# Norm statistics as wide products with a mean matrix, and products into a free bank before the first tile of each norm

## The reference

```python
def rms_norm(x, g):
    y = x * lax.rsqrt(jnp.mean(x * x, axis=-1, keepdims=True) + EPS)   # EPS = 1e-6
    return y * g

def modulate(h, shift, scale):
    return h * (1 + scale) + shift
```

## Time and profile before

| | |
|---|---|
| median of 3 runs | 3732.96 us (3728.23 to 3733.44) |
| profiled execution | 3734.95 us, span 3733.2 us |
| TensorE busy | 3505.1 us, 94% of the span |
| VectorE busy | 1916.7 us, 51% |
| ScalarE busy | 1265.7 us, 34% |
| GpSimd busy | 373.7 us, 10% |
| granted TensorE clock, mean | 0.966 of full |

### The profile page before, as it was taken

The page is one execution under the profiler, slowest core; times in us unless marked ns, Lnnn a source line. Parts: engine busy times, 40 slices in busy tenths (PEclk is TensorE's granted clock), DMA queues, the critical chain, the costliest instruction groups (busy, mean ns, idle before and its releaser), DMA issues.

```text
span 3733.2 us, 40477 instructions
## 1 busy us (share of the span) xinstructions
PE 3505.1 (94%) x17064; PEld 2896.1 (78%) x17064; DVE 1916.7 (51%) x2662; ACT 1265.7 (34%) x1779; POOL 373.7 (10%) x216
## 2 busy tenths in 40 slices
PE   2999999899979999999999999989999998999998
PEld 2888888788767888788777888766788876678887
DVE  8433343566656453635344333486564538656464
ACT  4322122444433222322234222334342432344242
POOL 3311001111110000000001000420100033010001
PEclk9999999899989999999999999989999999999999
DMA  5423241011115353535212232210232222012221
GB/s 193 141 80 123 85 152 63 29 35 35 34 63 174 124 198 113 190 122 176 89 66 96 92 101 96 82 53 6 68 106 97 96 74 75 6 52 98 99 96 57
DMA packets 95798, 348.83 MB, mean 93 GB/s; under 512 B 10624, under 2 KB 11136, under 8 KB 95104
## 3 DMA queue, kind: packets, MB, share of 16 engines
q1 hardware_dynamic: 94320, 343.06, 27.6%
q10 hardware_dynamic: 1296, 3.18, 0.2%
HBM read 344.10 MB, written 2.10 MB: 93 GB/s over the span
## 4 chain that ended last, share of the span: by engine, by line
PE 84%; DVE 9%; ACT 4%; POOL 1%; issue 1%; DMA 0%; SPq 0%; ACTq 0%; DVEq 0%; POOLq 0%
PE PS L341 83%; DVE CAC L1872 2%; ACT G L1111 1%; DVE ST L1679 1%; PE PS L413 1%; DVE WL L1448 1%; POOL SM L2160 1%; DVE SCR L1479 1%; ACT HH L994 1%; ACT G L982 1%; DVE PTL L1662 1%; DVE X L1843 0%; ACT PTH L1092 0%; DVE ST L1963 0%; DVE SCR L1471 0%
## 5 line engine op out<-in xcount | busy, mean ns | idle before, releaser
L341 PE MATMUL PS<-HH,WH 128*128 128x512 f32 (+1 forms) x3120 | 1194.4, 383 | 46.8 <-DVE HL L1560 21.1
L341 PE MATMUL PS<-HL,WH 128*128 128x512 f32 (+1 forms) x3120 | 1177.9, 378 | 0.0
L341 PE MATMUL PS<-HH,WL 128*128 128x512 f32 (+1 forms) x3120 | 1174.6, 376 | 0.0
L1448 DVE TENSOR_TENSOR WL<-RAW,WH 128x1024 fp32r<-128x1024 f32 x462 | 580.9, 1261 | 895.3 <-ACT WH L943 895.2
L943 ACT ACTIVATE WH<-RAW 128x1024 fp32r<-128x1024 f32 x496 | 523.2, 1057 | 1217.2 <-PE PS L341 1206.9
L341 PEld LDWEIGHTS PS<-HH,WH 128*128 128x128 f32 x3120 | 595.4, 191 | 164.0 <-DVE HL L1560 23.3
L341 PEld LDWEIGHTS PS<-HL,WH 128*128 128x128 f32 x3120 | 595.3, 191 | 109.4 <-issue 5.5
L341 PEld LDWEIGHTS PS<-HH,WL 128*128 128x128 f32 x3120 | 594.0, 190 | 108.7
L341 PE MATMUL PS<-AH,WH 128*128 128x512 f32 x1392 | 525.9, 378 | 1.7 <-DVE WL L1448 1.7
L341 PE MATMUL PS<-AL,WH 128*128 128x512 f32 x1392 | 525.5, 377 | 0.0
L341 PE MATMUL PS<-AH,WL 128*128 128x512 f32 x1392 | 523.8, 376 | 0.0
(11 more groups left out here) (277 smaller groups left out, 3288.2 us busy)
## 6 DMA issues: line engine op xcount, KB each, us to landing
RAW<-wst SPq DMA_DIRECT2D x640, 512.0 KB, 3.3
X<-xT SPq DMA_DIRECT2D x1, 2048.0 KB, 12.2
out<-X SPq DMA_DIRECT2D x8, 256.0 KB, 2.0
PTF<-cb SPq DMA_DIRECT2D x1, 1024.0 KB, 4.8
Y<-yT SPq DMA_DIRECT2D x1, 1024.0 KB, 6.9
PTF<-cb ACTq DMA_DIRECT2D x1, 1024.0 KB, 4.8
HM<-sg ACTq DMA_DIRECT2D x4, 256.0 KB, 3.7
ROPE<-rope SPq DMA_DIRECT2D x1, 512.0 KB, 4.5
```

Source lines behind the costliest of these rows:

```text
L341: return e.matmul(o, l, r, start=start, stop=stop)
L1448: e.tensor_tensor(lo, raw_block(s), f32(hi), ALU.subtract).then_inc(*did("dve_done", ("wlo", b)))
```

## The change

A constant column of 1/1024 (CST column 643), broadcast to 128x128, is the stationary matrix `mean`. A wide fp32 product of it with a tile of 512 or 768 tokens leaves the mean over the features on all 128 partitions at once. `means` issues such products, adding up in a bank:

- The one of ACC is put inside the last projection's tile m = 7, before its last input but one (`squares`). For f01 POOL adds only the squares of m = 1 to 3, and TensorE sums ACC and the other four. The one of G follows after m = 7, and after it `busy` issues three products with ROPE, a constant table, into a bank that nobody reads (bank 7, at f01 bank 1; none at f00).
- ACT takes the square root from the bank into ACC, with 1e-6 added; DVE takes the reciprocal on 128x512 or 128x768; DVE multiplies X by the gain column and by ACC in one instruction into G; ACT adds the bias and writes HH directly; DVE makes HL from G, bias and HH in one instruction. The POOL powers of the norms are gone.
- For layer norms `center` puts the product for the provisional mean before input 5 of tile m = 6 (4 in a mixer's projection), that of A2t before input 5 of m = 7, those of X(6) and ACC before input 10 (7 in a mixer's projection). DVE shifts X(6) before its own eviction. After m = 7 follow X(7), G, and four products with ROPE. ACT squares and copies the mean, DVE makes the variance, ACT the root, DVE the reciprocal; POOL subtracts the mean from X(1) to X(7) (1 to 5 at the end), which DVE did before.
- `prepare` loads the ACT tables early: 27 loads in the program.

The diff, cut to its core:

```diff
+        def means(name, src, N, step, start, stop, *more, into=None):
+
+            if start:
+                _, prior = take(name, N) if into is None else hold(name, N, into)
+                for p in prior:
+                    q.wait_ge(*p)
+            q.wait_ge(*step)
+            for c in range(0, N, 512):
+                d = min(c + 512, N)
+                m = mm(bank[name][:, c:d], mean, src[:, c:d], start, stop)
+            if stop:
+                more = ("tile", name), *more
+            if more:
+                m.then_inc(*did("pe_done", *more))
+
+        def busy(st, n):
+
+            bk, prior = hold(("busy", st), NX, 1 if st == "f01" else 7, ("busy", st))
+            for p in prior:
+                q.wait_ge(*p)
+            for i in range(n):
+                m = mm(bk, mean, ROPE[:, 0:512], True, True)
+            m.then_inc(*did("pe_done", ("busy", st)))
...
+        def squares(st):
+
+            up = BEFORE[st]
+            q.wait_ge("consts")
+            means(("ms", st), ACC, tokens(st), ("acc", up, 3 if up == "at" else 6), True, False, ("acc read", st),
+                  into=0 if up == "at" else 6)
+
         def norm(st):
-            up = BEFORE[st]
-            nt = 6 if wide(up) else 4
-            q.wait_ge("consts")
-            stat(st, [(ACC, 128, ones, ("acc", up, 6)), (G(("sq", up, 7)), 128, ones, ("sq", up, 7))], nt, 1,
-                 ("gdone", ("sq", up, 7)))
-            spread(st, nt, None, ("rs", st))
-            N = nt * 128
+            up, N = BEFORE[st], tokens(st)
+            for m in range(4, 8) if up == "at" else (7,):
+                means(("ms", st), G(("sq", up, m)), N, ("sq", up, m), False, m == 7, ("gdone", ("sq", up, m)))
+            if st != "f00":
+                busy(st, 3)
             return [(*hview(k, N), ("h", st, k), 128) for k in range(8)]
...
+        def center(st, m, at):
+
+
+            up = BEFORE[st]
+
+            def first():
+                means(("mean", st), ACC, NX, ("sum", st), True, True)
+
+            def second():
+                means(("v", st), A2t, NX, ("csq", st, 3), True, False, ("a2 read", st), into=7)
+
+            def third():
+                means(("d", st), X(6), NX, ("x", up, 6), True, False, into=6)
+                means(("v", st), ACC, NX, ("csq", st, 6), False, False, ("acc read", st))
+
+            return {6: {(at[0], 0): first}, 7: {(at[1], 0): second, (at[2], 0): third}}.get(m, {})
 
         def layer_norm(st):
...
+            means(("d", st), X(7), NX, ("x", BEFORE[st], 7), False, True)
+            means(("v", st), G(("ce", st, 7)), NX, ("csq", st, 7), False, True, ("gdone", ("ce", st, 7)))
+            if st != "end":
+                _, prior = hold(("busy", st), NX, 5, ("busy", st))
                 for p in prior:
                     q.wait_ge(*p)
+                for i in range(4):
+                    m = mm(bank["busy", st], mean, ROPE[:, 0:512], True, True)
+                m.then_inc(*did("pe_done", ("busy", st)))
             return [(*hview(k, NX), ("h", st, k), 128) for k in range(8)]
...
+            e.activation(ACC[:, 0:N], bank["ms", st][:, 0:N], ACT.Sqrt, bias=EP[:, 0:1]).then_inc(
+                *did("act_done", ("std", st), ("free", ("ms", st))))
+                a = e.activation(hi[:, 0:512], s[:, 0:512], ACT.Identity, bias=mcol(l, 3 * i, k, 0))
+                    a = e.activation(hi[:, 512:768], s[:, 512:768], ACT.Identity, bias=mcol(l, 3 * i, k, 1))
+                a.then_inc(*did("act_done", ("hhi", st, k)))
+                    part(upto[LAST[st]], 1)
...
+            q.wait_ge("tile", ("d", st))
+            q.wait_ge("a2 read", st)
+            e.activation(A2t[:, :], bank["d", st][:, :], ACT.Square).then_inc(*did("act_done", ("dsq", st)))
+            q.wait_ge("acc read", st)
+            e.activation(ACC[:, 0:512], bank["d", st][:, :], ACT.Copy).then_inc(*did("act_done", ("dcopy", st)))
+            q.wait_ge("var", st)
+            q.wait_ge("eps")
+            e.activation(A2t[:, :], A2t[:, :], ACT.Sqrt, bias=EP[:, 1:2]).then_inc(*did("act_done", ("std", st)))
...
+            q.wait_ge("std", st)
+            e.reciprocal(ACC[:, 0:N], ACC[:, 0:N]).then_inc(*did("dve_done", ("rs", st)))
+            q.wait_ge("rs", st)
+            spans = [(X, 0, 512, "x")] + ([(Y, 512, 768, "y")] if N > 512 else [])
+            for k in range(9):
+                    for s, (src, c, d, kind) in enumerate(spans):
+                        q.wait_ge(kind, up, k)
+                        e.scalar_tensor_tensor(out=G(use)[:, c:d], in0=src(k), scalar=mcol(l, 3 * i + 1, k, s), in1=ACC[:, c:d], op0=ALU.mult,
+                                               op1=ALU.mult).then_inc(*did("dve_done", ("nx" if d == N else "nxx", st, k)))
+                if k:
+                    use = ("n", st, k - 1)
+                    hi, lo = hview(k - 1, N)
+                    q.wait_ge("hhi", st, k - 1)
+                    for s, (src, c, d, kind) in enumerate(spans):
+                        e.scalar_tensor_tensor(out=lo[:, c:d], in0=G(use)[:, c:d], scalar=mcol(l, 3 * i, k - 1, s), in1=f32(hi)[:, c:d], op0=ALU.add,
+                                               op1=ALU.subtract).then_inc(*did("dve_done", *([("h", st, k - 1), ("gdone", use)] if d == N else [])))
+                if k >= 3:
+                    part(upto[LAST[st]], 1)
...
+        def shifted(st, k, done, *more):
+
+            c = -1024.0 / 768 / (ALPHA if st[0] == "c" else 1.0)
+            e.scalar_tensor_tensor(out=X(k), in0=bank["mean", st], scalar=c if k >= 6 else -1024.0 / 768, in1=X(k), op0=ALU.mult,
+                                   op1=ALU.add).then_inc(*did("dve_done", (done, st, k), *more))
+
+        def center(st, ready):
+
+            q.wait_ge("tile", ("mean", st))
+            q.wait_ge(*ready)
+            shifted(st, 6, "x-")
+            for k in range(4):
+                shifted(st, k, "cx")
+
+        def center_more(st, ready):
+
+            for k in (4, 5):
+                q.wait_ge("x", BEFORE[st], k)
+                shifted(st, k, "cx")
+            q.wait_ge(*ready)
+            shifted(st, 7, "x-", ("free", ("mean", st)))
...
         def layer_norm(st):
-            q.wait_ge("var", st)
-            q.wait_ge("pow half")
-            e.tensor_tensor(sm(("v", st), 16, 4), sm(("v", st), 12, 4), MH[:, 0:4], ALU.pow).then_inc(*did("pool_done", ("rs", st)))
+            q.wait_ge("dcopy", st)
+            for k in range(1, 8 if st != "end" else 6):
+                q.wait_ge(*(("cx", st, k) if k < 7 else ("x", BEFORE[st], 7)))
+                e.tensor_tensor(X(k), X(k), ACC[:, 0:512], ALU.subtract).then_inc(*did("pool_done", ("xs", st, k)))
```

More of the change, by code:

```diff
@@ L52 @@
 KS = (2, 3, 4, 5, 6, 0, 1, 7)
+AFTER = {before: stage for stage, before in BEFORE.items()}
 def wide(stage):
@@ L352, in lin @@
             K = len(xs)
+            for t in tiles:
+                upto["mid", t[0]] = allowed()
             for k, (hi, lo, step, rows) in enumerate(xs):
@@ L691, in fourier_out @@
             for m in range(4, 8):
[L692 to L712 removed]
+                lin([tile(m)], fx, None, {(6, 0): lambda: squares("f11")} if m == 7 else {})
@@ L909, in _ @@
         mods_on = True
-        xs = norm("f01")
-        ffn("f01", xs)
+        squares("f01")
+        ffn("f01", norm("f01"))
         ffn("f10", norm("f10"))
@@ L1018, in ffn @@
                 for m in range(8):
-                    if p == len(parts) - 1:
+                    last = p == len(parts) - 1
+                    if last and m == 7:
+                        stream(upto["mid", ("d", st, p, m)])
+                        prepare(ACT.Sqrt, "sqrt", AFTER[st])
+                    if last:
                         if st != "f11":
@@ L1196, in fourier @@
             for m in range(8):
+                if m == 7:
+                    prepare(ACT.Sqrt, "sqrt", "f11")
                 square("fo", m)
-                stream(upto["fw", m])
+                if m < 7:
+                    stream(upto["fw", m])
         def total(st, m):
@@ L1408, in _ @@
             square("in", m)
+        prepare(ACT.Sqrt, "sqrt", "f00")
         stream(upto["start"])
@@ L1585, in ffn @@
                         q.wait_ge("x", up, m)
-                    last = p == len(parts) - 1
                     steps = [("x", st, m)] if last else [] if N > 512 else [("xp", st, p, m)]
+                    if st == "f11" and last and m == 6:
+                        steps.append(("cx", "m0", 6))
                     if N == 512:
@@ L1849, in layer_norm @@
+            q.wait_ge("tile", ("v", st))
+            q.wait_ge("dsq", st)
+            e.tensor_tensor(A2t[:, :], bank["v", st][:, :], A2t[:, :], ALU.subtract).then_inc(*did("dve_done", ("var", st), ("free", ("v", st))))
+            shift(0)
+            q.wait_ge("std", st)
+            e.reciprocal(A2t[:, :], A2t[:, :]).then_inc(*did("dve_done", ("rs", st), ("free", ("d", st))))
+            q.wait_ge("rs", st)
```

(6 more changed lines are left out.)

279 lines of the change are left out of this document (127 added, 152 removed).

## The result

The changed kernel takes 3753.41 us (median of four, 3751.9 to 3753.92) for 3732.38 before: ratio 1.0055, 95% interval 1.0039 to 1.0071. It is 21 us slower; 3698 was forecast. The profiled execution took 3753.5 us, its span 3751.7. TensorE is busy for as long as before; VectorE has 46 us more.

A forecast was written before the change was run, and what follows sets the result against it. TensorE, busy 3505.1 of 3733.2 us, was taken as the bound, so only its idle or low-clock time could be won. Gains per norm summed to 35.0 us, 3734.95 to 3700, median 3698; range for 8 in 10: 3677 to 3728.

The forecast's parts named there:

- the reciprocal of 512 columns: In every norm's chain between Sqrt and first multiply: at most 1.2 us, at least 0.69, taken as 0.7.
- The rival built on it: Reciprocal's repeats not pipelined, an estimated 5 us per norm; at 8 ns more per column 3747 us; chance 0.05.
- the turning point of 5.7 ns a column: Reciprocal cost per column beyond the counted 1.4 ns from which the changed kernel turns slower than before.
- the 35 forecast: Total gain summed over all norms: 35.0 us.
- They cost nothing if the clock holds: RMS norms' three filler products end at 6.0 us, ahead of the first real product at 6.95, so cost nothing.
- 1.6 to 2.7 gained for each norm: Half the low-clock stretch behind first products saved: 1.6 us at f10 and fo, 2.6 at f11, 2.7 at m0.
- The forecast's first rival: Clock falls in spite of the filler, whose products take 2.07 us each: 3732, or 3741 us; chance 0.13.
- The layer norm's tail: Chain at m0, c0, m1 from eviction to difference: 8.35 us for 14.99, 14.82, 14.33 before.
- The in-line price at c0: Projection before c0: late sum and A2t, with the falling clock, cost 7.9 us more in line than before.
- The slow tiles behind m0: POOL's shifts slow DVE beside them: about 0.6 us behind on each of five tiles, 3 us lost.
- The square's 1.7: At RMS norms the square ends 1.67 us behind the last product, so the wide product starts from 1.7 on.
- f00's gain of 3: At f00 the first tile is ready near 75.2, not 78.3: 3 us gained, bounds 0 (all covered) and 6.

The follow-up runs named there:

- e1: Changed kernel with its eleven wide reciprocals replaced by a short tensor_scalar of the same shape; 3718.6 us.
- e3: Changed kernel with more filler products: 7 for 3 at narrow RMS norms, 9 at the wide one, 10 for 4 at layer norms; 3734.7 us.
- e12: Changed kernel with longer filler, mixers' mean subtraction before the weight split, A2t before the last input, and GpSimd's mean subtractions moved to VectorE; 3717.5 us.
- e5: Changed kernel with, in the mixers' projections, the mean subtracted before the weight split and A2t taken before the last input; 3734.3 us.
- e2: Changed kernel without the filler products at RMS and layer norms; 3748.8 us.
- e7: Changed kernel with all layer norms and their projections as in the kernel before, so wide RMS norms alone; 3727.0 us.
- e10: Wide RMS norms with longer filler and old layer norms, plus filler at four layer norms (one before X(7)'s sum, five behind the broadcasts); 3728.4 us.
- e15: Changed kernel with only A2t moved before the last input of the mixers' last tile; 3741.9 us.

## Why the prediction was wrong

**The step that failed first** is "the reciprocal of 512 columns stands in no row [...] at most 2 ns a column and 1.2 us [...] I take 0.7". It takes 3.34, and 4.95 for 768 columns: 6.3 ns a column (the slope between the two), not 2. The bound was no bound: it took the difference of two operations of 1 and 2 columns, 153 and 155 ns, which hardly rises with their size, for a price per column. The term is short by 2.65 us at nine norms and 4.05 at the wide one: 28 us of operations. In the gaps e1 gives back 16.1 us at the five RMS norms and 4.2 at the four layer norms before a projection, and at end nothing, since there GpSimd's subtractions take the reciprocal's place. The rule of the Trainium skill, "VectorE: DVE Perf Modes", "First, the fixed hardware budget" (an iterative divide with a repeat count of 8), was weighed against that row and laid aside; the estimate by it, 5 us (8 times 0.69 would be 5.5), was nearer than mine, and the measured 3.34 is 4.8 times the 0.69 of a plain operation of the shape. The rival built on it had a chance of 0.05 and the turning point of 5.7 ns a column beyond my 1.4; 4.9 beyond were measured, so that by this rival's own terms the kernel would have stayed about 5 us ahead. And with a short operation in its place the kernel takes 3718.6 (e1), 14 to 16 us ahead and not the 35 forecast. So there were further failures.

**"They cost nothing if the clock holds"**: it did not hold. The filler was reckoned to reach to within 1 us of the first product; with the reciprocal's 2.65 more, 4.01 us stand open, and the first stretch of the stage runs at 1.2 GHz as before or longer. In place of 1.6 to 2.7 gained for each norm, 1.0 was lost at f10, 0.8 at f01, 0.4 at fo, 1.1 gained at f11, and nothing at c0 and c1 (forty products 11.74 and 11.78 at c0): 14 us in all with m0. e1 (reciprocal short, filler unchanged: the clock stays at f01, f10 and f11) and e3 (reciprocal unchanged, filler long: it is 1.00 at all nine first products) show from both sides that it is the open time between filler and first product: 4.01 us at f10 in the changed kernel, 1.08 in e1, 0.58 in e3. The forecast's first rival, that the clock falls, is what happened in its effect, but not for its reason, and its fillers at 2.07 each did not occur at these norms.

**The layer norm's tail** was put at 8.35 and is 12.85 at m0, 12.60 at c0: beyond the reciprocal 1.9 and 1.6 us. The first multiply and difference stand beside GpSimd's subtractions (the difference takes 1.75 for 0.75), and a second multiply is in front of the first difference. The lock had been reckoned only for the tiles behind. e12 takes the subtractions off GpSimd and the gap at c0 falls by 1.3. By e1 this lock is worth more than these 1.9 and 1.6: with the reciprocal nearly gone the gap at m0 is still 12.0, so the two costs overlap, and the split between them is a way to book them.

**What came as forecast.** The in-line price at c0, 7.9 more than before, was 7.8 (shift +2.72 before the last two tiles, +10.54 at their end), and by the named cause: the wait for A2t behind a split that VectorE waited for; e5 shows it. The slow tiles behind m0 were put at 3: against 9.2 they are 3.9 late (13.06). The square's 1.7 and the chain of f10 without the reciprocal hold to 0.4 (e1). f00's gain of 3 was all covered, as its lower bound had it: the modulation gives the products at 110.11 for 110.14 before. Another 1.2 us is lost just behind them, where the granted clock up to 120.00 is 0.70 for 0.83; for that the forecast had no term.

**What none of it names.** At m0 and m1 the clock fell inside the mixer at two places where before it had not (1.6 and 1.9 us, 1.6 and 1.6). With these, and by the lengths of the operations, 28 + 14 + 7 (tails) + 4 (f00) + 7 make 60 for a miss of 53.5; 3.6 of the difference are terms that came out better (f01's products 1.2, the ACC product 0.87 for 1.06, in line at m0 and m1 1.4). The remaining 3 stay open. That the falls in the mixer depend on where its small gaps come to lie is argued, not shown; e2, e7 and the spread of e10 (23 us) show only that they change from kernel to kernel and from run to run.

## What to carry to other kernels

Don't extend a price from operations of one or two columns to one of 512: they show the fixed part only. If no row has the operation at that size, it is the first thing to bound by the dearest account of it, not by the row at hand. A filler is worth what it closes of the open time before the first real product: 4 us or more short of it, it was worth next to nothing here (e2), and with that closed 19 us, of which the norms themselves show 12 (e3). Work that is taken out of a serial chain into the products before it is gained only if its inputs are ready there: read what stands in front of them in each engine's row. And before a median is put down to an edit, compare the traces at the place of the edit: the clock elsewhere moved by 3 to 8 us from kernel to kernel (e2, e5, e7, e15).
